# The closing steps of the prompt pass take turns on two PSUM banks

## The reference, cut to what matters

```python
hp = hp + jnp.concatenate([pool_o, attn_o], axis=-1) @ w_out[l]
hp = hp + hier_moe(rms_norm(hp, norm_ffn_g[l]), *moe_args)
```

## Time and profile before

| | us |
|---|---|
| median of 3 executions | 1226.91 |
| lowest and highest | 1226.13, 1229.39 |
| the profiled execution's own time | 1225.94 |
| its span in the trace | 1224.1 |
| TensorE busy | 1085.3 (89%) |
| VectorE busy | 581.1 (47%) |
| ScalarE busy | 413.1 (34%) |
| GpSimd busy | 205.7 (17%) |

### The profile page before, as it was taken

The page is one execution under the profiler, slowest core; times in us unless marked ns, Lnnn a source line. Parts: engine busy times, 40 slices in busy tenths (PEclk is TensorE's granted clock), DMA queues, the critical chain, the costliest instruction groups (busy, mean ns, idle before and its releaser), DMA issues.

```text
span 1224.1 us, 16550 instructions
## 1 busy us (share of the span) xinstructions
PE 1085.3 (89%) x6208; PEld 732.9 (60%) x6208; DVE 581.1 (47%) x1282; ACT 413.1 (34%) x976; POOL 205.7 (17%) x256
## 2 busy tenths in 40 slices
PE   4999989899886999999997898499999999999920
PEld 2554433354343677777775556287878778788720
DVE  2234568999997777666462361213111111111138
ACT  1234445567534345555541333211111110111113
POOL 1432215354421000000012200000000000000032
PEclk9999999999988699999999899699999999999965
DMA  6510000010095911110012741499899999998757
GB/s 215 197 46 12 12 22 1 1 35 5 9 239 198 278 53 52 52 53 35 36 35 78 301 181 70 146 371 372 303 345 339 334 350 329 331 352 326 271 181 281
DMA packets 71372, 209.54 MB, mean 171 GB/s; under 512 B 11214, under 2 KB 31774, under 8 KB 61061
## 3 DMA queue, kind: packets, MB, share of 16 engines
q1 hardware_dynamic: 57119, 151.75, 35.1%
q0 software_dynamic: 10448, 44.21, 10.7%
q10 hardware_dynamic: 3742, 12.75, 2.7%
HBM read 171.40 MB, written 37.40 MB: 171 GB/s over the span
## 4 chain that ended last, share of the span: by engine, by line
PE 80%; DVE 9%; ACT 3%; DMA 3%; issue 2%; POOL 1%; SPq 0%; POOLq 0%; ACTq 0%; DVEq 0%; PEldq 0%
PE ps L1457 18%; PE ps L1463 10%; PE ps L1302 8%; PE ps L1091 5%; PE ps L1107 5%; PE ps L1118 5%; PE ps L1046 3%; PE ps L1079 3%; PE ps L1249 3%; PE ps L1260 2%; PE ps L1450 2%; PE ps L1272 2%; ACT mem L1533 2%; DVE mem L2002 2%; PE ps L1313 1%
## 5 line engine op out<-in xcount | busy, mean ns | idle before, releaser
L1533 ACT ACTIVATE mem<-ps 128x512 f32<-128x512 f32 (+10 forms) x376 | 172.6, 497 | 330.7 <-PE ps L1463 64.1
L1457 PEld LDWEIGHTS ps<-mem 128*128 128x128 f32 x2048 | 235.4, 193 | 16.8 <-issue 16.8
L1457 PE MATMUL ps<-mem 128*128 128x96 f32 x2048 | 234.9, 276 | 0.8 <-DVE mem L2404 0.8
L2002 DVE TENSOR_SCALAR_CACHE_REDUCE mem<-mem 128x768 bf16<-128x768 f32 (+2 forms) x134 | 166.5, 1283 | 0.0
L1302 PE MATMUL ps<-mem 128*128 128x256 f32 (+1 forms) x544 | 126.6, 385 | 5.8 <-ACT mem L1533 2.8
L1463 PE MATMUL ps<-mem 128*96 128x512 f32 x256 | 119.3, 609 | 2.4 <-DVE mem L2396 2.3
L1302 PEld LDWEIGHTS ps<-mem 128*128 128x128 f32 (+1 forms) x544 | 100.1, 189 | 23.1 <-ACT mem L1533 3.7
L2396 DVE TENSOR_TENSOR mem<-mem,ps 128x192 f32<-128x192 f32 x32 | 11.4, 356 | 212.7 <-ACT mem L1873 212.7
L1873 ACT ACTIVATE mem<-ps 128x192 f32<-128x192 f32 x32 | 10.6, 333 | 264.0 <-PE ps L1457 264.0
L983 POOL DMA_INDIRECT mem<-xn_rows,mem x32 | 29.0, 905 | 369.4 <-PE ps L1450 317.6
L1463 PEld LDWEIGHTS ps<-mem 128*96 128x96 f32 x256 | 39.6, 164 | 58.5 <-issue 52.4
(11 more groups left out here) (292 smaller groups left out, 1387.2 us busy)
## 6 DMA issues: line engine op xcount, KB each, us to landing
mem<-in_expert_w_gate SPq DMA_DIRECT2D x32, 1024.0 KB, 5.5
mem<-in_expert_w_up SPq DMA_DIRECT2D x32, 1024.0 KB, 8.7
mem<-in_expert_w_down SPq DMA_DIRECT2D x32, 1024.0 KB, 10.9
expert_rows<-mem ACTq DMA_DIRECT2D x32, 384.0 KB, 8.0
expert_rows<-mem SPq DMA_DIRECT2D x2, 4608.0 KB, 30.3
mem<-in_x_prompt SPq DMA_DIRECT2D x16, 512.0 KB, 4.3
mem<-in_w_in SPq DMA_DIRECT2D x3, 2048.0 KB, 10.8
h_rows<-mem SPq DMA_DIRECT2D x8, 512.0 KB, 2.6
```

Source lines behind the costliest of these rows:

```text
L1457: ins = mm(ps[:, 2 + s, j * CAP:(j + 1) * CAP], wgu[w][:, j // 2, k, (j % 2) * P:(j % 2 + 1) * P], xgT[:, s, k, :], start=(k == 0), stop=( ...
L1533: return fn(out, in_, ACT.Copy, scale=scale)
L2002: v.tensor_scalar(bufs[a % 3][0:R, 0:w], sc, mid[:, a:a + 1], None, ALU.is_ge, ALU.add, accum_out=cnt[:, a:a + 1]).then_inc(step, 1)
```

## The change

The TensorE tasks of the closing alternate between buffer `PT1` (bank 5) and `M` (bank 7): OP 6.3 on PT1, OT 7 on M, OP 7.0 on PT1, OP 7.1 on M, XR 6.0 on PT1, OP 7.2 on M, XR 6.1 on PT1, OP 7.3 on M, LG 6 on PT1, OP 8.0 on M, OP 8.1 on PT1, XR 7.0 on M, OP 8.2 on PT1, XR 7.1 on M, OP 8.3 on PT1, LG 7 on M. The order of the tasks, the instructions and their sizes stay. All places that named bank 7 or the semaphores of `M` for these tasks now look the buffer up. The core of the diff:

```diff
+        in_turn = {}
+
         def part_of(t):
-            return "PT0" if t == ("OP", NT, 5) else "M"
+            return "PT0" if t == ("OP", NT, 5) else in_turn.get(t, "M")
+
+        def bank_of(t):
+            return P2B[part_of(t)]
...
+        tasks += closing
+        for n, t in enumerate([t for t in closing if t[0] not in ("SQ", "NM")]):
+            in_turn[t] = ("PT1", "M")[n % 2]
...
                 claim(pe, "2b", part_of(t), t)
+                bank_ = bank_of(t)
...
-                            copied(pe, "2b", "M", ("OT", i))
+                            copied(pe, "2b", part_of(("OT", i)), ("OT", i))
...
-                        ins = mm(ps[0:r, 7, 0:256], lhs, wout[:, k, 256 * t[2]:256 * t[2] + 256], start=(k == 0), stop=(k == last))
+                        ins = mm(ps[0:r, bank_, 0:256], lhs, wout[:, k, 256 * t[2]:256 * t[2] + 256], start=(k == 0), stop=(k == last))
...
-                    copied(pe, "2b", "M", ("XR", i, 1))
+                    copied(pe, "2b", part_of(("XR", i, 1)), ("XR", i, 1))
...
-                ins.then_inc(filled["2bM"], 1)
+                ins.then_inc(filled["2b" + part_of(t)], 1)
...
-                    take(act, "2b", "M", t)
-                    copy(x2T[:, 4 * t[2]:4 * t[2] + 4, 0:r], four(ps[:, 7, :], r)).then_inc(emptied["2bM"], 1)
+                    take(act, "2b", part_of(t), t)
+                    copy(x2T[:, 4 * t[2]:4 * t[2] + 4, 0:r], four(ps[:, bank_of(t), :], r)).then_inc(emptied["2b" + part_of(t)], 1)
...
-                    v.tensor_tensor(part, ps[0:r, 7, 0:256], part, ALU.add).then_inc(emptied["2bM"], 1)
+                    v.tensor_tensor(part, ps[0:r, bank_of(t), 0:256], part, ALU.add).then_inc(emptied["2b" + part_of(t)], 1)
```

More of the change, by code:

```diff
@@ L484, in program @@
         i = NT - 1
-        tasks += [("OP", i - 1, 3), ("SQ", i - 1), ("OT", i), ("OP", i, 0), ("NM", i - 1), ("OP", i, 1), ("XR", i - 1, 0),
-                  ("OP", i, 2), ("XR", i - 1, 1), ("OP", i, 3), ("LG", i - 1), ("SQ", i), ("OP", NT, 0), ("NM", i), ("OP", NT, 1),
-                  ("XR", i, 0), ("OP", NT, 2), ("XR", i, 1), ("OP", NT, 3), ("LG", i)]
+        closing = [("OP", i - 1, 3), ("SQ", i - 1), ("OT", i), ("OP", i, 0), ("NM", i - 1), ("OP", i, 1), ("XR", i - 1, 0),
+                   ("OP", i, 2), ("XR", i - 1, 1), ("OP", i, 3), ("LG", i - 1), ("SQ", i), ("OP", NT, 0), ("NM", i), ("OP", NT, 1),
+                   ("XR", i, 0), ("OP", NT, 2), ("XR", i, 1), ("OP", NT, 3), ("LG", i)]
+        tasks += closing
+        for n, t in enumerate([t for t in closing if t[0] not in ("SQ", "NM")]):
+            in_turn[t] = ("PT1", "M")[n % 2]
         tasks_elsewhere = list(tasks)
@@ L1285, in tail @@
                     for c in range(4):
-                        ins = tr(ps[:, 7, c * P:(c + 1) * P], inv_wide[:, c * P:(c + 1) * P], ident(P))
+                        ins = tr(ps[:, bank_, c * P:(c + 1) * P], inv_wide[:, c * P:(c + 1) * P], ident(P))
                 elif kind == "OP":
@@ L1295, in tail @@
                         for k in range(4):
-                            ins = mm(ps[0:r, 7 if t[2] == 4 else 4, :], mixS[:, k, :], wout[:, 4 + k, half], start=(k == 0), stop=(k == 3))
+                            ins = mm(ps[0:r, bank_, :], mixS[:, k, :], wout[:, 4 + k, half], start=(k == 0), stop=(k == 3))
                         ins.then_inc(filled["2b" + part_of(t)], 1)
@@ L1306, in tail @@
                         c = 4 * t[2] + j
-                        ins = tr(ps[:, 7, j * r:(j + 1) * r], x2[0:r, i % 2, c * P:(c + 1) * P], ident(r))
+                        ins = tr(ps[:, bank_, j * r:(j + 1) * r], x2[0:r, i % 2, c * P:(c + 1) * P], ident(r))
                 elif kind == "LG":
-                    copied(pe, "2b", "M", ("XR", i, 1))
+                    copied(pe, "2b", part_of(("XR", i, 1)), ("XR", i, 1))
                     if i == 0:
@@ L1312, in tail @@
                     for k in range(KC):
-                        ins = mm(ps[0:r, 7, 0:36], x2T[:, k, 0:r], rw[:, k, :], start=(k == 0), stop=(k == KC - 1))
+                        ins = mm(ps[0:r, bank_, 0:36], x2T[:, k, 0:r], rw[:, k, :], start=(k == 0), stop=(k == KC - 1))
                 elif kind == "RK":
@@ L1752, in tail @@
                         act.wait_ge(x2_out[s], 16 * (i // 2))
-                        take(act, "2b", "M", ("XR", i - 2, 1))
+                        take(act, "2b", part_of(("XR", i - 2, 1)), ("XR", i - 2, 1))
                     if i == NT:
@@ L2148, in route @@
                 if i < NT:
-                    v.tensor_tensor(L8[0:r, i, :], ps[0:r, 7, 0:36], bias36[0:r, :], ALU.add).then_inc(emptied["2bM"], 1)
+                    t = ("LG", i)
+                    v.tensor_tensor(L8[0:r, i, :], ps[0:r, bank_of(t), 0:36], bias36[0:r, :], ALU.add).then_inc(emptied["2b" + part_of(t)], 1)
                     return
@@ L2272, in tail @@
                 if kind == "OT":
-                    take(dve, "2b", "M", t)
+                    take(dve, "2b", part_of(t), t)
                     dve.wait_ge(o_kept, i + 1)
                     if i:
-                        take(dve, "2b", "M", ("OP", i - 1, 3))
-                    v.tensor_tensor(mixA[:, :, :].rearrange("p b q -> p (b q)"), ps[:, 7, :], Osb, ALU.mult).then_inc(emptied["2bM"], 1)
+                        take(dve, "2b", part_of(("OP", i - 1, 3)), ("OP", i - 1, 3))
+                    v.tensor_tensor(mixA[:, :, :].rearrange("p b q -> p (b q)"), ps[:, bank_of(t), :], Osb, ALU.mult)\
+                        .then_inc(emptied["2b" + part_of(t)], 1)
                 elif kind == "OP":
@@ L2281, in tail @@
                         part = hbS[:, 2 * (t[2] - 4):2 * (t[2] - 3), :]
-                        new = ps[0:r, 7 if t[2] == 4 else 4, :].rearrange("p (q n) -> p q n", q=2)
+                        new = ps[0:r, bank_of(t), :].rearrange("p (q n) -> p q n", q=2)
                         v.tensor_tensor(part, new, part, ALU.add).then_inc(emptied["2b" + part_of(t)], 1)
```

## The result

| | us |
|---|---|
| median before (4 executions) | 1227.09 |
| median after (4 executions) | 1218.22 |
| ratio of the executions, after to before | 0.9923, 95% interval 0.9906 to 0.9940 |
| profiled execution before, after | 1225.94, 1217.78 |
| span before, after | 1224.1, 1215.9 |

The change saves 8.9 us by the medians; by the interval, between 7.4 and 11.5. On another chip, later, the same kernel stood at 0.9938 (0.9921 to 0.9955) of the kernel before, 7.6 us. The forecast was 8.1.

A forecast was written before the change was run, and what follows sets the result against it. TensorE bounds the kernel, idle 9.0 us of the closing while taking turns with its readers. Removed waits of 9.8 less 1.7 of remaining waits save 8.1 us: 1226.9 - 8.1 = 1218.8, range 1215.5 to 1222.2.

The forecast's parts named there:

- Distances: Closing's start-to-start step distances: shorter ones remove OP 3.15, XR 3.36, decode OP 2.60, LG 0.68, OT nothing; sum 9.8 us.
- NM 6: DVE's norm ahead of XR 6.0: still ends at 651.04, held up by GpSimd's mask, so XR 6.0 waits 1.3 us.
- the rival that gave NM 6 free 0.15: NM 6 isn't held up by its earlier start, ends at 650.1 or before; gain 9.0 to 9.4, 1217.7; chance 0.15.
- The rule on NM 6: Skill's rule: DVE's norm blocks until GpSimd's SBUF-reading instruction finishes; taken exactly, NM 6 ends at 651.92, whatever its start.
- Later waits: Closing: XR 7.0 waits 0.2 us for NM 7; OP 7.3 and OP 8.3 wait 0.1 each; LG 7 starts at 669.9.
- Cover: GpSimd's wait for the store of tile 7's `x2`: cover shrinks from 11 to some 7 us, store stays hidden.
- Clock: TensorE's clock behind the closing: zero taken; transposes may win 1.6 us at most, first expert's products 2.1 either way.
- Slower: Clock falls to half level when the closing starts in two banks and stays there; some 1250 us; chance 0.03.
- Part eaten: Closing's steps don't pipeline, or a clock fall in its last decode quarters leaves 4.5 to 5.5 us; 1222; chance 0.10.
- nothing gained: Next stage is set by something else, a transfer or GpSimd late by 8 us; 1226.9; chance 0.05.

The follow-up runs named there:

- the kernel with the mask later: The change, and GpSimd begins its mask only when NM 6 (tile 6's norm on DVE) is done; median 1215.22 us, 0.9908 of the kernel before.
- the late `mixA` wait: The change, and OP 7.0 waits for `mixA` only ahead of its fifth of eight matmul pairs; median 1217.73 us, 0.9935 of the kernel before.
- the kernel with both edits and three banks: The change plus GpSimd's mask behind NM 6, OP 7.0's later wait for `mixA`, and turns on banks 5, 7, 4; 1214.00 us, 0.9907 of before.

## Why the prediction was right

The forecast was 1218.8, within 1215.5 to 1222.2; measured 1218.22. The mechanism held: 8.1 us were forecast for the closing and 7.94 came. That the two medians lie within 0.6 us is in part luck, since the code ahead of the closing alone varied by 3.3 us between traces. Its steps, with the trace of after shifted by the 1.1 us that LG 5 came late:
- **Distances.** OP to the next step 3.60 forecast, 641.95 - 638.41 = 3.54 measured; XR to OP 0.50, and 0.47 in tile 6, 0.57 and 0.58 in tile 7; decode quarter to the next 1.8, and 668.62 - 666.75 = 1.87; OT to OP 1.54, and 1.48. LG to OP 1.93, and 1.80 twice. TensorE's busy time in the closing was to stay about as before; it fell from 33.6 to 31.7 (637.7 to 680.3, and 638.4 to 673.5), since the groups overlap.
- **NM 6.** XR 6.0 was to start at 651.1: 652.29 - 1.1 = 651.2. The value taken (it ends with GpSimd) was right; the lower bound (1.29 long) and the value between (3.24 from its earlier start) were not, and the rival that gave NM 6 free 0.15 falls with them. The wait itself was sized too small, 1.3 against 1.72: the steps in front were faster than taken, and since NM 6's end doesn't move, TensorE waited the difference. So two errors cancelled here, and they had to. For the same reason the price of a free norm was low: set free, it gave 1.6, where the rival had 0.9 to 1.3.
- **The rule on NM 6.** The Trainium skill ("SBUF — State Buffer", Who interferes with whom) has the later of the two instructions blocked until the first has finished. The end that doesn't depend on the start agrees with it at all four starts. That it would then need its full 1.29 does not: the measured end was 0.40 to 0.43 behind GpSimd's in the trace. For planning, the measured distance counts.
- **Later waits.** XR 7.0 forecast at 665.1, measured 665.1; LG 7 at 669.9, measured 670.0. OP 7.3 waits as forecast for OP 7.2's reader (0.69 behind XR 6.1, forecast 0.60).
- **Cover.** The store of tile 7's `x2` was issued at 666.07 and GpSimd passed `prompts_done` at 673.71, on TensorE: 7.6 us of cover, where some 7 were worked out, and enough.
- **Clock.** Zero was taken. It came out as 0.9 us faster transposes, nearly all waited away at the key gather, and 1.2 lost near 750. What the step missed is the gather: 12.6 us from issue to the first matmul that needs it, whatever the clock does in front. The upper value of 1.6 could never have been had: in the kernel with the mask later the first transposes did run at full clock throughout, in 5.67 (5.7 was worked out), and the transposes behind the gather still started 14.51 behind LG 7's reader, against 14.48 with the change and 14.66 before.
- **Slower.** The rival of a clock that falls inside the closing needed a reason, and bank turns are none: 1.00 throughout the changed kernel's closing. But a fall did happen there once, behind a wait of 2.51 us (the late `mixA` wait), and cost 1.7. The Trainium skill ("TensorE: Matmul & The Clock Gate", A second HAM failure mode) names cycling through PSUM banks as what made the clock of a kernel fall and rise. That isn't borne out here: of ten traces with turns of two or three banks, nine kept 1.00 through the closing.
- **Part eaten, nothing gained.** From LG 7's reader to the first expert's products it was 795.70 - 679.92 = 115.78 before and is 788.72 - 673.09 = 115.63, so in these two executions the closing's 7.94 arrived whole.

## What to carry to other kernels

When the trace shows producer and reader taking strict turns with both engines mostly free, count the turns: each single buffer costs the reader, two handoffs and the producer's own pipeline end, together some 0.5 to 0.9 us here, and the second buffer takes nearly all of it where the next step's data are ready. Before promising the sum, walk the steps again with the new distances and look for instructions that were long but hidden: here one norm of 3.24 us, harmless before, became the largest wait, and moving a mask on another engine was worth another 1.6 us only after the change. An edit that merely starts work earlier in front of such a wait gains nothing; here the one trace of it even lost 1.7 by the clock. The same goes for what lies behind: a faster start of the next stage is worth nothing where that stage waits for a transfer.

## What the runs showed of the hardware

A VectorE instruction with two SBUF inputs (128x1024) and a GpSimd instruction of 9.3 us side by side: the first took 3.24, 3.73, 4.46 and 5.25 us by its start, alone 1.29, and ended 0.40 to 0.43 behind the other in all eight traces that have the pair. VectorE instructions beside it with one input from PSUM kept their 0.42 and 0.69. GpSimd's instruction kept its 9.3.

It holds the other way round as well: GpSimd's next, short instruction takes 0.20 alone (in the kernel with the mask later), but 0.40 when it comes while NM 6 still runs, as in the kernel before. In the kernel with both edits and three banks it came 0.18 behind the start of NM 7, took 1.16, and ended 0.05 behind it, by its timeline:

```profile
658.05 1.29 DVE L2310 SCALAR_TENSOR_TENSOR mem<-mem 128x1024 f32<-128x1024 f32 x1
658.23 1.16 POOL L968 TENSOR_SCALAR mem<-mem 64x8 bf16<-64x8 bf16 x1
```

In the closing, TensorE's clock stayed at 1.00 over an idle stretch of 1.72 us (four traces) and fell to 0.50 behind one of 2.51 (one trace), with dense work on both sides. The length of one wait doesn't decide it: behind LG 7, where TensorE waited 0.70 to 0.81, the clock fell in eight of the thirteen traces and stayed at 1.00 in five, and these five had waited 0.70 as well. So both show what can happen, and neither is a limit.
